# Moving the state-space output matrix to VectorE, the chunk load ahead of the query weights, and the state-space output products ahead of the last gate group

## What is computed

```python
z = h @ w_in
u, q, kvc, kvs, kvw, g_nsa, g_a, g_b = jnp.split(z, cuts, axis=-1)
y_ssm, ssm_state = s5_scan(u, h0, lam_re, lam_im, log_dt, b_re, b_im, c_re, c_im, d_skip)
zg = jax.nn.gelu(y_ssm)
glu = zg * jax.nn.sigmoid(zg @ w_glu + b_glu)
...
o_nsa = nsa_attention(qh, gh, full_c, full_s, win_ext, ...)
merged = sigmoid(g_a) * (glu @ w_ssm_out) + sigmoid(g_b) * (o_nsa @ w_nsa_out)
```

## Time and profile before

| | |
|---|---|
| median of the runs shown | 816.21 us |
| lowest and highest | 814.77 and 816.44 us |
| span of the profiled execution | 820.2 us |
| TensorE busy | 789.7 us (96%) |
| VectorE, ScalarE, GpSimd busy | 345.2, 193.6, 138.9 us |
| mean granted TensorE clock | 0.992 |

### The profile page before, as it was taken

How to read it: one execution, slowest core, us unless ns; L and a number is a source line. 1 busy time by engine, 2 the same in 40 slices (tenths; PEclk the granted TensorE clock), 3 DMA queues, 4 the chain that set the end, 5 groups by cost and what they waited for, 6 DMA issues and landing times. The chain is left out here.

```text
span 820.2 us, 13714 instructions
## 1 busy us (share of the span) xinstructions
PE 789.7 (96%) x5151; PEld 513.4 (63%) x5151; DVE 345.2 (42%) x944; ACT 193.6 (24%) x462; POOL 138.9 (17%) x167
## 2 busy tenths in 40 slices
PE   8999999999999999898999999999999999999995
PEld 6455577877778879655666775445556564554441
DVE  2279911365553332666734363123732101115433
ACT  3010211311111344554523200035211111122222
POOL 3029300500001211234510100012111101014000
PEclk9999999999999999999999999999999999999998
DMA  9540294551411396800030179003699999996011
GB/s 323 146 123 0 81 280 164 145 46 40 172 44 43 109 175 225 225 1 2 1 117 2 59 219 370 2 26 116 226 420 414 418 417 416 416 353 206 26 51 39
DMA packets 81221, 136.49 MB, mean 166 GB/s; under 512 B 33926, under 2 KB 57546, under 8 KB 76946
## 3 DMA queue, kind: packets, MB, share of 16 engines
q1 hardware_dynamic: 64636, 110.17, 40.9%
q0 software_dynamic: 3728, 13.38, 4.6%
q10 hardware_dynamic: 12798, 12.12, 4.4%
HBM read 116.55 MB, written 21.19 MB: 168 GB/s over the span
## 5 line engine op out<-in xcount | busy, mean ns | idle before, releaser
L1170 PE MATMUL ps<-hT,w_slot 128*128 128x288 f32 x640 | 156.2, 407 | 0.0
L1170 PEld LDWEIGHTS ps<-hT,w_slot 128*128 128x128 f32 x640 | 121.3, 190 | 34.1 <-issue 0.8
L1170 PE MATMUL ps<-w_slot,hT 128*128 128x512 f32 (+1 forms) x320 | 127.0, 555 | 0.3 <-DVE hT L1835 0.3
L1170 PEld LDWEIGHTS ps<-w_slot,hT 128*128 128x128 f32 x320 | 60.0, 190 | 61.0 <-issue 42.4
L1170 PE MATMUL ps<-w_slot,merged 128*128 128x512 f32 x128 | 55.9, 593 | 0.0
L1674 PE MATMUL ps<-w_slot,hT 128*32 128x256 f32 x544 | 49.7, 380 | 0.0
L2624 DVE SCALAR_TENSOR_TENSOR th<-th,ps 128x256 f32<-128x256 f32 x12 | 5.1, 422 | 105.2 <-ACT th L2077 105.2
L1170 PEld LDWEIGHTS ps<-w_slot,merged 128*128 128x128 f32 x128 | 24.0, 190 | 28.4 <-issue 28.2
L1043 POOL TENSOR_TENSOR hT<-hT,w_p 128x512 f32<-128x512 f32 (+3 forms) x11 | 25.1, 2282 | 51.2 <-DVE w_p L2150 51.2
L1170 PE MATMUL ps<-qg,w_slot 128*128 128x288 f32 x128 | 33.7, 408 | 0.0
L1674 PEld LDWEIGHTS ps<-w_slot,hT 128*32 128x32 f32 x544 | 26.3, 110 | 10.0 <-issue 2.3
(11 more groups left out here) (441 smaller groups left out, 1223.1 us busy)
## 6 DMA issues: line engine op xcount, KB each, us to landing
merged<-in_w_exp_down SPq DMA_DIRECT2D x11, 1024.0 KB, 17.1
w_slot<-in_w_in SPq DMA_DIRECT2D x8, 1024.0 KB, 6.9
wgu<-in_w_exp_gate SPq DMA_DIRECT2D x8, 1024.0 KB, 12.8
wgu<-in_w_exp_up SPq DMA_DIRECT2D x8, 1024.0 KB, 15.1
w_slot<-in_w_exp_gate SPq DMA_DIRECT2D x8, 1024.0 KB, 13.1
w_slot<-in_w_exp_up SPq DMA_DIRECT2D x8, 1024.0 KB, 15.6
expert_rows<-onsaT ACTq DMA_DIRECT2D x12, 512.0 KB, 8.0
w_slot<-in_w_exp_down SPq DMA_DIRECT2D x5, 1024.0 KB, 16.1
```

Of the source, the lines that this page charges most:

```text
L1170: ins = pe.matmul(out, a, b, start=(n == 0), stop=(n == len(pairs) - 1))
```

## The change

It does five things. `gm` is made on VectorE behind `vn`, by six operations, and no longer on GpSimd. The load of `uc` is issued ahead of the query weights and of the outputs. Only one gate group stands ahead of `x`; group 1 comes behind `d`, ahead of the other query products; its staging buffer lies in `vt` instead of `xg`, so the waits for the stores move from `x` to `vt`. The `y` products stand ahead of the last gate group, which takes the place of `keep_busy(12)`. The weights `g2` and `glu` are loaded behind the Toeplitz loads, and `glu` ahead of `g3`.

```diff
-KD_A = 3
+KD_A = 1
@@ make_plan
     for i in range(6):
         p.add(("d", i), "dve" if i % 2 else "act")
+    gate_jobs(p, KD_A)
     for m in range(1, GQA):
         for h in range(2):
             p.add(("q", m, h), "act")
-    for m in range(KD_A, KD):
+    for m in range(KD_A + 1, KD - 1):
         gate_jobs(p, m)
     for i in range(8):
         p.add(("y", i), "dve")
+    gate_jobs(p, KD - 1)
@@ buffers
-            stage_a = xg_t[:, 0:8 * HALF].rearrange("p (b w n) -> p b w n", b=4, w=2)
+            stage_a = vt[:].rearrange("p a b -> p (a b)")[:, 0:8 * HALF].rearrange("p (b w n) -> p b w n", b=4, w=2)
@@ SyncE
             load_weights("g0")
             load_weights("g1")
+            sp.wait_ge(u_out, 16 * NT)
+            sp.wait_ge(v_made, 1)
+            sp.wait_ge(g_made, 1)
+            sp.dma_start(uc, u_dram.rearrange("(c t) n -> c t n", t=CH)).then_inc(uc_ld, 16)
             load_weights("q")
...
-            sp.wait_ge(u_out, 16 * NT)
-            sp.wait_ge(v_made, 1)
-            sp.wait_ge(g_made, 1)
-            sp.dma_start(uc, u_dram.rearrange("(c t) n -> c t n", t=CH)).then_inc(uc_ld, 16)
-
...
-            load_weights("g2")
...
             for t in range(CH):
                 sp.dma_start(wt[GRP * t:GRP * t + GRP, :, GRP * t:P], k_dram[:, :, 0:P - GRP * t]).then_inc(w_toep, 16)
+            load_weights("g2")
+            load_weights("glu")
             load_weights("g3")
-            load_weights("glu")
@@ GpSimd
-            pool.wait_ge(powers, 1)
-            pool.wait_ge(*emptied(("c", 1)))
...
-            link(pool.tensor_tensor(gm[:, 0], pr, cr, ALU.mult))
-            link(pool.tensor_tensor(tg9, pi, ci, ALU.mult))
-            link(pool.tensor_tensor(gm[:, 0], gm[:, 0], tg9, ALU.subtract))
-            link(pool.tensor_tensor(gm[:, 1], pi, cr, ALU.mult))
-            link(pool.tensor_tensor(tg9, pr, ci, ALU.mult))
-            link(pool.tensor_tensor(gm[:, 1], gm[:, 1], tg9, ALU.add))
-            pool.tensor_scalar(gm[:, 1], gm[:, 1], -1.0, None, ALU.mult).then_inc(g_made, 1)
@@ TensorE
+            gate_products(KD_A)
             for m in range(1, GQA):
                 for h in range(2):
                     query_products(m, h)
-            for m in range(KD_A, KD):
+            for m in range(KD_A + 1, KD - 1):
                 gate_products(m)
...
-            keep_busy(12)
+            gate_products(KD - 1)
@@ ScalarE
-            act.wait_ge(u_out, 16 * NT)
             for m in range(KD_A):
                 take_gates(m, stage_a)
-            for b in range(4):
-                act.wait_ge(tg_out[b], 16 * gates_out(b, 2 * KD_A))
...
             take_query(0, 0)
+            for b in range(2 * KD_A):
+                act.wait_ge(tg_out[b], 16 * gates_out(b, 2 * KD_A))
...
+            act.wait_ge(pe_done, PLAN.done(("x", 4)))
+            take_gates(KD_A, stage_b)
             for m in range(1, GQA):
                 for h in range(2):
                     take_query(m, h)
-            act.wait_ge(pe_done, PLAN.done(("x", 4)))
-            for m in range(KD_A, KD):
+            for m in range(KD_A + 1, KD - 1):
                 take_gates(m, stage_b)
...
+            take_gates(KD - 1, stage_b)
@@ VectorE
-            dve.tensor_copy(pwr[:, 0], pw[:, CH - 1]).then_inc(powers, 1)
-            for j in range(1, CH):
+            for j in range(CH):
                 dve.tensor_copy(pwr[:, j], pw[:, CH - 1 - j])
...
+            tt(gm[:, 0], pr, c_re, ALU.mult)
+            link(tt(tg9, pi, c_im, ALU.mult))
+            tt(gm[:, 0], gm[:, 0], tg9, ALU.subtract)
+            link(tt(gm[:, 1], pi, c_re, ALU.mult))
+            link(tt(tg9, pr, c_im, ALU.mult))
+            dve.scalar_tensor_tensor(gm[:, 1], gm[:, 1], -1.0, tg9, ALU.mult, ALU.subtract).then_inc(g_made, 1)
...
-            for b in range(4):
-                dve.wait_ge(tg_out[b], 16 * gates_out(b, 2 * KD_A))
             for i in range(0, 5, 2):
                 o = take(("x", i))
...
+            for b in range(2 * KD_A):
+                dve.wait_ge(tg_out[b], 16 * gates_out(b, 2 * KD_A))
             for i in range(1, 8, 2):
                 o = take(("vt", i))
```

More of the change, by code:

```diff
@@ L595, in build @@
         dt_done, angles, trig = sem("dt_made"), sem("angles_made"), sem("sin_cos_made")
-        powers, v_made, g_made = sem("powers_made"), sem("v_made"), sem("g_made")
+        v_made, g_made = sem("v_made"), sem("g_made")
         ucg_made = sem("u_by_groups")
@@ L2269, in _ @@
             tt(v8[1], v8[1], u8, ALU.add).then_inc(v_made, 1)
+            n9 = [P, NS, CH + 1, GRP]
+            pr, pi = (pw[:, :, r, :].rearrange("p t s -> p s t").unsqueeze(3).broadcast_to(n9) for r in range(2))
+            c_re, c_im = (cst[:, r].unsqueeze(2).broadcast_to(n9) for r in range(2))
+            tg9 = tmp_g.rearrange("p (s t c) -> p s t c", s=NS, t=CH + 1)
+            tt(gm[:, 0], pr, c_re, ALU.mult)
[4 more added lines that the diff above has]
+            dve.scalar_tensor_tensor(gm[:, 1], gm[:, 1], -1.0, tg9, ALU.mult, ALU.subtract).then_inc(g_made, 1)
             dve.wait_ge(gates_made, NT)
```

## The result

The changed kernel took 843.58 us (median of 4, 842.74 to 844.23) where the kernel before, beside it on the same chip, took 816.33 (median of 4, 814.77 to 817.54). The ratio is 1.0316, with an interval of 1.0289 to 1.0342. The forecast was 839, the range 830 to 846.

What follows compares the result with a forecast made beforehand. TensorE's order was taken to bound the kernel, with SyncE's chain already without spare cover. Chain +15.2, query wait +5.3, clock +1.0 and +1.7 gave +23.2 us: 839 us against the median 816.21, range 830 to 846.

Steps and rivals of the forecast that it cites:

- The chain: SyncE's loads and stores after the last gate group, up to ScalarE's first attention drain: start 15.2 us later, cover used up.
- The 2.10 us behind `y`: Empty transposes and idle after y on TensorE: removed by the change, but swallowed by the longer wait for SyncE's chain.
- Rival 3: Faster: chain not binding, gain behind y stays, first stall vanishes; 813 us, chance 0.04.
- The query weights: Delayed on the queue by uc to 119.2 us, so TensorE's query (0, 0) waits 5.3 us (3.6 to 7).
- `uc` in time by 0.9 us: Load ahead of x: transfer taken as 4.3 us, copy ready at 111.0, TensorE wants x at 111.9.
- The clock behind the first stall: Lower granted clock after the wait at query (0, 0): costs 1.0 us (0 to 1.5).
- The second stall: TensorE idle at least 10 us before attention's remaining transposes and pre; low clock there costs 1.7 us, chain no shorter.
- Rival 1: Query weights come in time, beside the moved load or by queue slack; 833 us, chance 0.14.
- Rival 2: uc itself late because g_made on VectorE is late; at 105 it costs 7 us more, 846 us, chance 0.07.
- Rival 4: Clock costs its full price in both stalls, +0.5 and +3.3 over the sum; 843 us, chance 0.15.
- Span against median: Whole kernel: profiled execution before taken as 4.0 us above its median, so span 843.4 became 839.4 against the median 816.21.
- Output matrix to VectorE: Six operations moved from GpSimd: g_made near 91 us, covered by SyncE's wait for kv until 96.41; costs nothing.

Runs made afterwards that it cites:

- E1: Changed kernel with the y products behind the last gate group again, followed by twelve filling transposes; 827.51 us, ratio 1.0105.
- E3: Changed kernel with SyncE's loads and stores around the last gate group reordered, state stores ahead of most pages and part of w1; 825.47 us, ratio 1.0071.
- E9: Changed kernel with the 16 page numbers read into registers ahead of the wait for the last gate group; 833.59 us, ratio 1.0183.
- E6: Kernel before the change with only SyncE's chain reordered as in E3; 818.90 us, ratio 1.0008.
- E4: Changed kernel with two gate groups ahead of x and E3's reordered chain; 823.99 us, ratio 1.0054.
- E10: Changed kernel with two gate groups ahead of x, E3's order and E9's page numbers in registers; 821.42 us, ratio 1.0027.
- E12: E10's kernel unchanged, one more execution profiled to look into its spread; 819.09 us.
- E5: Changed kernel with 44 empty transposes on TensorE ahead of its wait for the query weights; 842.07 us, ratio 1.0306.

## Why the prediction was right, and where it was off

**The chain: right.** The step on which most of the sum rested was that `y`'s length, 15.2 us, reappears in full in SyncE's chain because its cover was used up. SyncE's chain starts 25.3 us late, 15.2 of it from this; at `pre`, without the earlier start, E1, E3 and E9 bring back 15.7, 16.4 and 9.6 us by three edits that leave the rest of the change in place, and E6 shows the cover in the kernel before. The 2.10 us behind `y` were swallowed as foreseen. Rival 3, faster, needed a short chain and no first stall: E4 and E10 have both, and their best executions reach 815 and 814 where it said 813; their medians, 824 and 821, do not. The changed kernel is not that kernel.

**The query weights: right in kind; the size came out by luck.** 5.50 us measured, 5.3 forecast. But both ends of the wait were forecast 2 us too early: `x` was to be done at 113.9 and was at 115.8, the weights were to be there at 119.2, with 121 as the bound, and TensorE went on at 121.32. The forecast moved the weights by `uc`'s 4.3 us; their last packet ended 6.6 us later than in the kernel before (120.81 against 114.24), about as long as `uc` really took. In the kernel before these weights had 30 us of slack and TensorE never waited for them.

**`uc` in time by 0.9 us: wrong, late by 1.9.** The failing term is its transfer, "I take 4.3, between the two". VectorE's copy started at 111.25, not 108.5. The data moved from 103.27 to 110.24, 7.0 us: more than the bound of 5.3 from the rows, and more than the 4.7 us of the estimate from the Trainium skill (DMA: Bandwidth & Descriptors, section "Why a DMA increments its semaphore by 16 and not by 1"). Another 1.0 us passed until the copy started, where 0.2 was allowed. The trace agrees with the twelve engines of that estimate, in that twelve packets were under way for most of the time. Both sums failed in the rate: they rested on what all transfers together move, 221 to 339 GB/s, while these 1.18 MB in 7.0 us are 169 GB/s. 72 packets by twelve are six turns, and six times 1.13 us are 6.8. Beside them the queue did not fill up with query weights; SyncE's issuing of those 16 loads stretched to 19.85 us. Why it stretched, and why one packet takes 1.13 us, no run isolates.

**The clock behind the first stall: 1.0 forecast, 2.7 measured.** The window that I sized it by, 0.62 over 4 us, I put down to half-idle work; it looks more like the stretches that come in some executions and not in others (E10 to E12), and it was no measure for a stall. Here the clock stayed at 0.50 from 116.5 to 126.7 us, through nearly all of the wait and the first 5.4 us of the query product, so that the product paid for most of its length; E5 gives 2.7 us back. The upper bound of 1.5 was too low. The Trainium skill (TensorE: Matmul & The Clock Gate, Part 1: The HAM clock gate) has the half rate as the rule after an idle stretch; the trace agrees, with 0.50 in both stalls.

**The second stall: 1.7 forecast, 1.2 measured, and a chain 1.8 shorter than assumed.** The low clock cost 1.2 us on the transposes before `pre`. The prediction held the chain to be no shorter than before; it was, by 0.8 us from its first issue to its last and by 1.0 from there to ScalarE's drain, for a reason that no run isolates.

Up to `pre` the working gave 23.2 against 24.7 measured: 1.9 (`uc`), 0.2 (query wait) and 1.7 (first clock) were missed, and 2.3 (0.5 and 1.8) were too much behind the chain's start.

**The other rivals.** Rival 1, query weights in time, fell with the wait of 5.50 us. Rival 2, a late `g_made`, fell with `gm` done at 89.35. Rival 4 named 843 us, the nearest number to the 843.58 measured, but not for its reason: the first stall cost 2.7 us where it had 1.5, and the second 1.2 where it had 5.

**Span against median: a step outside the kernel.** I set the profiled execution 4.0 us above its median; it was 5.7. That of the changed kernel was 0.7 above its own. The profiled execution of before also had two of the stretches of low clock (336 and 376 us, 0.62 and 0.57 granted over 4 us) that E10 to E12 show to come and go. The forecast difference of spans was 23.2, the measured one 22.3; the medians differ by 27.2, so the forecast came out 4 short. That the two stretches, and a start 1.3 to 1.7 us later than in most profiles, explain most of the 5.7 is argued, not shown. Against the difference of the medians the working itself is 4.0 too low; that it agrees with the spans within 0.9 is in part the luck of which executions were profiled.

**Output matrix to VectorE: right, nothing.** `gm` was ready at 89.35, forecast 91, behind a cover that ended at 97.15. The 30 us came back because seven small VectorE operations no longer lasted as long as the GpSimd operations beside them. This part was not run alone, nor were the order of `uc` and the query weights and the later loads of `g2` and `glu`; for the last, no wait for these weights is in the changed kernel's timeline.

## What to carry to other kernels

When work is moved ahead of a milestone, list every engine that starts something at that milestone: here TensorE's order was neutral, and the cost was the length of the moved piece, paid through a queue that TensorE had waited for by no more than 1.05 us. A chain without slack is worth reordering before anything is moved: put the transfer that another engine waits for ahead of the bulk. And a load that is pulled forward on a shared queue delays all behind it by its own time, so ask of each of them by when it is wanted. That time is the load's own, 7.0 us here, and not what the rate of the whole queue would make of it.

## What the runs showed of the hardware that was not expected

- A page load with its register read takes 17.20 / 16 = 1.07 us of SyncE's time, with the numbers read ahead 8.24 / 16 = 0.51. Half of the page loads' issue time was the read.
- Beside each of the seven large GpSimd operations one small VectorE operation lasted until the GpSimd operation ended (within 0.5 us): these seven took 4.08 to 5.46 us instead of 0.17. A mean over such a group (8.96 / 7 = 1.28 us) describes none of its members. Moving the GpSimd work to VectorE made VectorE less busy, 329.0 us instead of 345.2, with twelve large operations instead of six.
- The load of 72 rows of 16 KB had twelve packets under way at a time and moved at 169 GB/s, where 347 to 386 GB/s had been moved in the 4 us before.
- Behind the 5.50 us stall the clock stayed low for 10.2 us in all, through 5 us of uninterrupted products. With 44 empty transposes in that place, the low stretch still came, for 3.4 us.
- The same kernel, the same waits and the same work are run with low clock in one execution and with full clock in the next (E10, E12, at 370 us). The stretch made eight score products 1.37 us longer; a difference of that size between two profiles need not be an effect of an edit.
